# Input x in eight pieces handled ahead of the weights, with idle products on TensorE, in a one-core transformer block

## The reference, cut to what matters

```
h = rmsnorm(x, g_mix);  z = h @ w_in                 # 2048 x 14848 columns in nine groups
o_a = gated linear recurrence (16 heads);  o_b = sliding-window attention (32 heads, 4 key heads)
x = x + concat(sigmoid(gate_a)*o_a, sigmoid(gate_b)*o_b) @ w_out
x = x + square(relu(rmsnorm(x, g_mlp) @ w_up)) @ w_down
x = x + sigmoid(x @ w_ple_gate) * (p @ w_ple_proj)
out = rmsnorm(x, g_final)
```

## Time and profile before

| | |
|---|---|
| median of the runs shown | 1722.49 us |
| the profiled execution's own time | 1721.62 us |
| its span, first to last instruction | 1719.9 us |
| TensorE busy | 1698.4 us, 99% |
| VectorE busy | 1105.5 us, 64% |
| ScalarE busy | 925.2 us, 54% |
| mean rate of the DMAs | 183 GB/s |

### The profile page before, as it was taken

One profiled execution on the slowest core, in us unless ns is written; L12 is line 12 of the kernel. 1 busy time (PEld: TensorE's weight loads), 2 busy tenths in 40 slices (PEclk: granted clock), 3 DMA queues, 4 the chain that ended last, 5 costly groups with the idle time before them and its releaser, 6 DMA issues.

```text
span 1719.9 us, 23521 instructions
## 1 busy us (share of the span) xinstructions
PE 1698.4 (99%) x8685; PEld 1416.6 (82%) x8685; DVE 1105.5 (64%) x1409; ACT 925.2 (54%) x1227; POOL 17.2 (1%) x72
## 2 busy tenths in 40 slices
PE   7999999999999999999999999999999999999997
PEld 6887887788887888878888888888888888888886
DVE  6667866875668756687585565655555556566565
ACT  6566646655566555655546544445454545454454
POOL 3000000000000000000000000000000000000000
PEclk9999999999999999999999999999999999999999
DMA  6665555566655566655556666666666666665654
GB/s 221 204 176 172 173 176 165 172 178 178 184 179 168 179 175 186 178 171 174 180 174 214 184 195 185 195 187 195 191 190 192 190 190 192 188 192 187 183 182 137
DMA packets 163293, 315.35 MB, mean 183 GB/s; under 512 B 10161, under 2 KB 10482, under 8 KB 163058
## 3 DMA queue, kind: packets, MB, share of 16 engines
q1 hardware_dynamic: 162016, 312.01, 60.1%
q10 hardware_dynamic: 1170, 1.87, 0.3%
HBM read 311.74 MB, written 2.10 MB: 182 GB/s over the span
## 4 chain that ended last, share of the span: by engine, by line
PE 96%; ACT 2%; DVE 1%; DMA 0%; issue 0%; SPq 0%; ACTq 0%; DVEq 0%
PE acc L681 21%; PE acc L682 21%; PE acc L687 21%; PE acc L695 6%; PE turn L695 6%; PE turn L682 3%; PE turn L687 3%; PE turn L681 3%; PE turn L701 3%; PE acc L701 3%; PE turn L723 2%; ACT w_hi L982 0%; PE turn L774 0%; ACT pr L1035 0%; PE turn L750 0%; PE turn L821 0%
## 5 line engine op out<-in xcount | busy, mean ns | idle before, releaser
L1339 DVE TENSOR_TENSOR w_lo<-w_raw,w_hi 128x1024 fp32r<-128x1024 f32 x588 | 719.8, 1224 | 562.0 <-ACT w_hi L982 559.3
L982 ACT ACTIVATE w_hi<-w_raw 128x1024 fp32r<-128x1024 f32 x588 | 622.7, 1059 | 705.8 <-PE acc L687 448.3
L681 PE MATMUL acc<-w_hi,hT 128*128 128x512 f32 x1104 | 436.0, 395 | 3.9 <-DVE hT L1379 3.9
L682 PE MATMUL acc<-w_hi,hT 128*128 128x512 f32 x1104 | 431.1, 391 | 0.0
L687 PE MATMUL acc<-w_lo,hT 128*128 128x512 f32 x1104 | 295.4, 389 | 0.0
L681 PEld LDWEIGHTS acc<-w_hi,hT 128*128 128x128 f32 x1104 | 207.9, 188 | 47.8 <-ACT w_hi L982 5.1
L687 PEld LDWEIGHTS acc<-w_lo,hT 128*128 128x128 f32 x1104 | 207.4, 188 | 43.6
L682 PEld LDWEIGHTS acc<-w_hi,hT 128*128 128x128 f32 x1104 | 208.0, 188 | 41.8
L681 PE MATMUL acc<-w_hi,mT_hi 128*128 128x512 f32 x416 | 164.4, 395 | 0.0
L682 PE MATMUL acc<-w_hi,mT_lo 128*128 128x512 f32 x416 | 162.2, 390 | 0.0
L695 PE MATMUL acc<-hT,w_hi 128*128 128x512 f32 x448 | 140.2, 394 | 0.0
(11 more groups left out here) (250 smaller groups left out, 1552.2 us busy)
## 6 DMA issues: line engine op xcount, KB each, us to landing
w_raw<-in_w_in_dram SPq DMA_DIRECT2D x232, 512.0 KB, 3.7
w_raw<-in_w_up_dram SPq DMA_DIRECT2D x128, 512.0 KB, 3.7
w_raw<-in_w_down_dram SPq DMA_DIRECT2D x128, 512.0 KB, 4.6
w_raw<-in_w_out_dram SPq DMA_DIRECT2D x64, 512.0 KB, 3.9
w_raw<-in_w_ple_gate_dram SPq DMA_DIRECT2D x32, 512.0 KB, 4.0
x_sb<-in_x_dram SPq DMA_DIRECT2D x8, 256.0 KB, 7.3
w_raw<-in_w_ple_proj_dram SPq DMA_DIRECT2D x4, 512.0 KB, 4.1
out_dram<-x_sb SPq DMA_DIRECT2D x6, 256.0 KB, 3.1
```

The costliest lines, as they stand in the source:

```text
L681: pe.matmul(a, hi[:, k, t, :], w_hi[:, s, kk, :], start=first and kk == 0, stop=False)
L682: pe.matmul(a, lo[:, k, t, :], w_hi[:, s, kk, :], start=False, stop=False)
L982: act.activation(w_hi[:, n % W_SLOTS], w_raw[:, n % RAW_SLOTS], ACT.Copy)\
L1339: dve.tensor_tensor(w_lo[:, n % W_SLOTS], w_raw[:, n % RAW_SLOTS], w_hi[:, n % W_SLOTS].bitcast(F32), ALU.subtract).then_inc(w_lo_ready, 1)
```

## The change

x comes in eight pieces of 256 columns, both halves of the rows in one DMA of 256 KB (rows of 1 KB). SP sends piece 0 first, then the weights of chunk 0, pieces 1 and 2, the weights of chunk 1, piece 3, and so on. The two small rows move from SP to ACT's queue, so that hgrn_norm_g's row is issued fourth there. TensorE makes five idle products (128 x 128 float32, identity times identity, into a PSUM tile that is free) ahead of its wait for `rows`, and eight more between the turn of piece 0 and chunk 0. Piece 1 is turned in the middle of chunk 0, between the four products of its first 128 rows and the four of its second; piece n+1 ahead of chunk n for n = 1 to 6. The transposes are 32 as before. ACT rounds piece 0 ahead of `w_hi` of chunk 0, and piece n+1 behind `w_hi` of chunk n. DVE weights and subtracts piece 0 ahead of `w_lo` of chunk 0, weights piece 1 behind it, and for n = 1 to 6 weights piece n+1 ahead of `w_lo` of chunk n and subtracts it behind. One piece is as many elements as one (block, t) was: eight operations of each kind, as before.

```diff
+PIECES = 8
+PIECE = D_MODEL // PIECES
...
-            sp.dma_start(rows[0:16, :], g_mix[0]...)
-            sp.dma_start(rows[16:32, :], g_mlp[0]...)
+            def load_x(i):
+                cs = slice(i * PIECE, (i + 1) * PIECE)
+                sp.dma_start(x_sb[:, :, cs], x_rows[:, :, cs]).then_inc(x_landed[i], 16)
             load_x(0)
             for slot in HEAD:
                 load(slot)
-                if slot[0] in (1, 2, 3):
-                    load_x(slot[0])
+                if slot[0] == 0:
+                    load_x(1)
+                if slot[0] + 2 < PIECES:
+                    load_x(slot[0] + 2)
...
# TensorE, in chunk()
+                if kind == "kv":
+                    pe.wait_ge(hT_ready, c + 1)
                 for kk in range(2):
+                    if n == 0 and kk == 1:
+                        pe.wait_ge(x_landed[1], 16)
+                        x_piece_turn(1)
...
+            def idle_products(n):
+                for _ in range(n):
+                    pe.matmul(acc[1][1][:, 0:P], ident[:], ident[:], start=True, stop=True)
             pe.wait_ge(ident_made, 1)
+            idle_products(5)
             pe.wait_ge(rows_landed, 16 * 4)
             pe.transpose(bank(("rows",))[:, 0:P], rows[:], ident[:])
             for slot in HEAD:
-                (two turns ahead of chunks 0, 1, 2 and 4)
+                if n == 0:
+                    pe.wait_ge(x_landed[0], 16)
+                    x_piece_turn(0)
+                    idle_products(8)
+                elif n + 1 < PIECES:
+                    pe.wait_ge(x_landed[n + 1], 16)
+                    x_piece_turn(n + 1)
                 chunk(slot)
...
# ScalarE
+            act.dma_start(rows[0:16, :], g_mix[0]...)
             act.dma_start(rows[32:64, :], lb_logits...)
+            act.dma_start(rows[16:32, :], g_mlp[0]...)
             act.wait_ge(rows_filled, 1)
             act.dma_start(rows[64:65, :], hgrn_norm_g)
...
             for slot in HEAD:
+                if slot[0] == 0:
+                    x_piece_hi(0)
                 split_hi(slot)
-                if slot[0] in (0, 2, 4, 6): (x_hi for t = 0 and 1)
+                if slot[0] + 1 < PIECES:
+                    x_piece_hi(slot[0] + 1)
...
# VectorE
             for slot in HEAD:
-                if slot[0] in (0, 2, 4, 6): (x_weighted for t = 0 and 1)
+                if slot[0] == 0:
+                    x_piece_weighted(0)
+                    x_piece_lo(0)
+                elif slot[0] + 1 < PIECES:
+                    x_piece_weighted(slot[0] + 1)
                 split_lo(slot)
-                if slot[0] in (0, 2, 4, 6): (x_lo for t = 0 and 1)
+                if slot[0] == 0:
+                    x_piece_weighted(1)
+                if slot[0] + 1 < PIECES:
+                    x_piece_lo(slot[0] + 1)
```

More of the change, by code:

```diff
@@ L217, in sem @@
             return ctx.enter_context(nc.semaphore(name))
-        x_landed = [[sem(f"x_landed{t}{cb}") for cb in range(4)] for t in range(TT)]
+        x_landed = [sem(f"x_landed{i}") for i in range(PIECES)]
         rows_filled = sem("rows_filled")
@@ L419, in program @@
         use(("rows",), 3, cols_ready, 1)
-        for cb in range(4):
-            for t in range(TT):
-                use(("xT", cb, t), t + 2 * (cb % 2), tmp_full, 2 * cb + t + 1)
+        for i in range(PIECES):
+            use(("xT", i), i % 4, tmp_full, i + 1)
         for t in range(TT):
@@ L536, in _ @@
         def _(sp):
[L537 to L543, removed]
+            x_rows = x[0].rearrange("(t p) d -> p t d", p=P)
+            def load_x(i):
+                cs = slice(i * PIECE, (i + 1) * PIECE)
+                sp.dma_start(x_sb[:, :, cs], x_rows[:, :, cs]).then_inc(x_landed[i], 16)
             load_x(0)
@@ L674, in chunk @@
                     return
+                if kind == "kv":
+                    pe.wait_ge(hT_ready, c + 1)
                 for kk in range(2):
                     k = 2 * c + kk
+                    if n == 0 and kk == 1:
+                        pe.wait_ge(x_landed[1], 16)
+                        x_piece_turn(1)
                     for t in range(TT):
-                        if kind == "kv" and c % 2 == 0 and kk == 0:
-                            pe.wait_ge(hT_ready, 2 * (c // 2) + t + 1)
                         a = acc_of(kind, j, col, t)[:]
@@ L727, in x_turn, with x_piece_turn @@
                 turn((stage, cb, t), lambda i: x_sb[:, t, (4 * cb + i) * P:(4 * cb + i + 1) * P])
+            def x_piece_turn(i):
+                turn(("xT", i), lambda q: x_sb[:, q % 2, (2 * i + q // 2) * P:(2 * i + q // 2 + 1) * P])
+            def idle_products(n):
+                for _ in range(n):
+                    pe.matmul(acc[1][1][:, 0:P], ident[:], ident[:], start=True, stop=True)
             def head_turn(kind, j, hp, src):
@@ L957, in _ @@
             chain = Chain(act, "act_chain")
+            act.dma_start(rows[0:16, :], g_mix[0].rearrange("(h p) -> h p", p=P)).then_inc(rows_landed, 16)
             act.dma_start(rows[32:64, :], lb_logits.rearrange("a (h p) -> (a h) p", p=P)).then_inc(rows_landed, 16)
+            act.dma_start(rows[16:32, :], g_mlp[0].rearrange("(h p) -> h p", p=P)).then_inc(rows_landed, 16)
             act.wait_ge(rows_filled, 1)
@@ L987, in sum_squares @@
                 for half in range(2):
-                    if stage == 0:
-                        act.wait_ge(x_landed[t][2 * half], 16)
-                        act.wait_ge(x_landed[t][2 * half + 1], 16)
+                    if stage == 0 and t == 0:
+                        for i in range(4 * half, 4 * half + 4):
+                            act.wait_ge(x_landed[i], 16)
                     act.activation(squares, x_sb[:, t, half * 1024:(half + 1) * 1024], ACT.Square,
@@ L1007, in x_hi, with x_piece_hi @@
                    .then_inc(hi_done, 1)
+            def x_piece_hi(i):
+                act.wait_ge(tmp_full, i + 1)
+                act.activation(hT_hi[:, 2 * i:2 * i + 2], tmp[:, i % 2].rearrange("p (k t c) -> p k t c", k=2, t=TT),
+                               ACT.Copy).then_inc(hi_done, 1)
             def z_out(kind, j, dst, done, func=ACT.Copy, scale=R):
@@ L1301, in _ @@
             for slot in HEAD:
+                if slot[0] == 0:
+                    x_piece_hi(0)
                 split_hi(slot)
-                if slot[0] in (0, 2, 4, 6):
-                    for t in range(TT):
-                        x_hi(0, slot[0] // 2, t)
+                if slot[0] + 1 < PIECES:
+                    x_piece_hi(slot[0] + 1)
                 act.wait_ge(w_hi_ready, slot[0] + 1)
@@ L1364, in x_weighted @@
             def x_weighted(stage, cb, t):
-                name = ("xT" if stage == 0 else "x1T", cb, t)
+                name = ("x1T", cb, t)
                 dve.wait_ge(full(name), nth(name))
@@ L1380, in x_lo, with x_piece_weighted, x_piece_lo @@
                                   ALU.subtract).then_inc(hT_ready, 1)
+            def x_piece_weighted(i):
+                name = ("xT", i)
+                dve.wait_ge(full(name), nth(name))
+                if i >= 2:
+                    dve.wait_ge(hT_ready, i - 1)
+                g = cols[:, 2 * i:2 * i + 2].unsqueeze(2).to_broadcast([P, 2, TT * P])
+                dve.tensor_tensor(tmp[:, i % 2].rearrange("p (k c) -> p k c", k=2),
+                                  bank(name)[:].rearrange("p (k c) -> p k c", k=2), g, ALU.mult).then_inc(tmp_full, 1)
+            def x_piece_lo(i):
+                dve.wait_ge(hi_done, i + 1)
+                ks = slice(2 * i, 2 * i + 2)
+                dve.tensor_tensor(hT_lo[:, ks], tmp[:, i % 2].rearrange("p (k t c) -> p k t c", k=2, t=TT),
+                                  hT_hi[:, ks].bitcast(F32), ALU.subtract).then_inc(hT_ready, 1)
             def rotate(src, dsts, t, heads, ta, tb):
@@ L1770, in _ @@
             for slot in HEAD:
-                if slot[0] in (0, 2, 4, 6):
-                    for t in range(TT):
-                        x_weighted(0, slot[0] // 2, t)
+                if slot[0] == 0:
[3 more added lines that the diff above has]
+                    x_piece_weighted(slot[0] + 1)
                 split_lo(slot)
-                if slot[0] in (0, 2, 4, 6):
-                    for t in range(TT):
-                        x_lo(0, slot[0] // 2, t)
+                if slot[0] == 0:
+                    x_piece_weighted(1)
+                if slot[0] + 1 < PIECES:
+                    x_piece_lo(slot[0] + 1)
                 dve.wait_ge(w_lo_ready, slot[0] + 1)
```

## The result

| | before | after |
|---|---|---|
| median of 12 runs each | 1722.78 us (1721.59 to 1725.18) | 1726.29 us (1725.63 to 1729.41) |
| the profiled execution | 1721.62 us, span 1719.9 | 1728.20 us, span 1726.4 |
| ratio, 95% interval | | 1.0023 (1.0016 to 1.0031) |

The forecast was 1721.5 us, in 1718.5 to 1723.7, with 0.04 on slower by over 0.2%. The kernel is slower by 0.23%. The two profiled executions differ by more than the medians (6.6 against 3.5 us): the one of before lies 1.2 us under its median, the one of after 1.9 above. So traces show places, and medians what a place is worth.

A forecast was written before the change was run, and what follows sets the result against it. TensorE, busy 99%, was taken as the bound. Chunk 0 at 9.45 plus 28.35 put chunk 8 at 37.8 against 38.32, gain 0.5: 1721.62 - 0.5 = 1721.1, with half the run's offset 1721.5 us, range 1718.5 to 1723.7.

The forecast's parts named there:

- The likeliest case: Whole kernel: chunk 8 starts at 37.8 against 38.32, gain 0.5, time 1721.5 us; chance 0.47.
- The rows: Start: hgrn_norm_g's row, issued fourth on ACT at 2.28, takes 2.5 and is there at 4.8.
- rival B: Start: the rows land late behind x and the weights, chunk 0 starts 2.2 later, 1723.7 us; chance 0.11.
- S: Start of chunk 0 on TensorE, forecast 9.45 us, set by the idle products, against 11.89 before.
- point of decision: Start: if the rows land at 5.8 or later, the kernel is slower than before.
- The clock: Chunk 0: the clock rises at 9.4, 3.5 us after the eight idle products begin at 5.9; gained 1.6.
- The ties: Chunks 0 to 8: ACT and DVE lose their lead, TensorE waits; 3.92 + 3.17 + 9.96 + 11.3 = 28.35 us.
- restart: TensorE after a stall: restarting its pipeline, bounded by 0 and 0.16 each, 1.3 for eight stalls; taken as 0.
- rival A: Chunks 0 to 8: TensorE runs without gaps, 24.9 us, gain 4.0, 1718.1 us; this or most of it 0.12.
- The loop: Behind the start of chunk 8: nothing is changed, so the two kernels are compared there.
- half carry: Whole time: the profiled run is 0.87 under the median; half is carried over, from 1721.1 to 1721.5.

The follow-up runs named there:

- rows_first: Changed kernel with g_mix's and g_mlp's rows sent by SyncE ahead of x again; 1726.33 us, 1.0021 of the kernel before.
- before_idle: Kernel before with only the 13 idle products added, five ahead of its wait for the rows, eight ahead of chunk 0; 1722.39 us, 0.9996.
- before_8: Kernel before with eight idle products between the first turns and chunk 0, none ahead of the rows; 1721.00 us, 0.9990.
- no_idle: Changed kernel without its 13 idle products; 1727.51 us, 1.0025 of the kernel before.
- lead_rows_8: Changed kernel with small rows sent first, pieces turned one chunk earlier, and only the eight idle products ahead of chunk 0; 1719.45 us, 0.9981 of the kernel before.
- lead_rows_8_late: lead_rows_8 with ScalarE's sums of squares and the three small steps that depend on them one slot later; 1720.92 us, 0.9987 of the kernel before.
- lead_one: Changed kernel with pieces 2 and 3 turned ahead of chunk 1, then piece n+2 ahead of chunk n; 1725.14 us, 1.0013 of the kernel before.
- lead_rows: Changed kernel with small rows sent first and pieces turned one chunk earlier, all 13 idle products kept; 1720.78 us, 0.9988 of the kernel before.
- after_8: Changed kernel without the five idle products ahead of the rows, the eight kept; 1725.42 us, 1.0015 of the kernel before.

## Why the prediction was wrong, step by step

The likeliest case had chunk 8 0.5 us earlier than before; it came 3.7 us later (first records, 41.89 for 38.16). Of its steps:

- **The rows: the largest error of one term.** "I take 2.5: 4.8" was 4.4 us, and TensorE turned the rows at 6.80: 2.0 us late, of which 1.7 show at chunk 0's first record (11.19 for 9.45; by the chain, 11.54, it is 2.1). This is rival B, at nearly its full price (S = 11.7), and its point of decision (a landing at 5.8) held. I gave it 0.11. The reason for 2.5, that "the row is one short line", was wrong: TensorE waits for all four small DMAs, 65 lines, and the change sends them side by side with x and the first weights. The bounds of the term (4.1 to 7.0) held it; the row nearest in kind, a small DMA issued amid x and weights at 2.28, was the sinks' 4.7. rows_first shows the cause. The Trainium skill (DMA: Bandwidth & Descriptors, Queues, rings and completion order) says that each of the 16 engines takes turns between the queue rows that have work. By that rule a small DMA on ScalarE's queue shares its engines with SyncE's backlog; the trace agrees, with 44 packets of q10 beside 452 of q1, and 4.4 us behind a backlog and 1.8 without.
- **The clock.** "It comes at 9.4: chunk 0 is warm" was 12.15 by the trace's clock reading, 4.2 us after the eight began and not 3.5: two of chunk 0's products ran at the low level, 0.3 us by the chain (0.5 by the records, which give that much less to the rows). The mechanism held (before_idle, before_8, no_idle against the changed kernel).
- **The ties: mechanism right, size low.** Chunk 0 to 1 took 4.44 for 3.92 (the clock), 1 to 2 3.34 for 3.17, 2 to 5 10.86 for 9.96, 5 to 8 12.06 for 11.3. The last two are 1.7 us too little. I had DVE start 0.09 after the turn, by the chain; it starts 0.70 after the turn's first record, as in before (17.10 after 16.41), and that is 0.34 after chunk n's first record (22.94 after 22.60). And a stall costs a restart, which I set at 0: chunk 8 takes 2.85 us behind its wait in lead_rows_8 and 2.72 without it in lead_rows_8_late, 0.13 for one stall by the records. By the chain it is 0.27, since the first step behind the wait is 0.50 and not 0.23. The bound was 0.16. The waits are where the prediction put them: w_lo in chunks 2 to 5, w_hi ahead of 6, 7 and 8. lead_one and lead_rows show that they hang on the lead. With the clock up in each from the first or second product, chunks 0 to 7 take 24.7 us in before_8, 25.6 in lead_rows_8 and 30.2 in after_8: the ties cost some 5 us, where the prediction had 3.4 (28.35 less rival A's 24.9).
- **The loop.** "I compare the two kernels at the start of chunk 8, since behind it nothing is changed" failed. The traces lose 2.64 us more at the loop's two turns, about 2 of it against a usual trace; in medians five idle products more are worth 0.9 to 1.4, part of it start. No rival had it. That it depends on the number of idle products ahead of the loop, and not on the x order, the early clock or the size of the program, is shown. That TensorE waits there for instructions that are fetched anew, where a block of them ends at an unlucky place of the loop's head, fits the second gap closely: its end follows the "instruction" packet, and its place moves with the records ahead of it. But no run moved the loop's head by anything else than idle products or looked for the gap at a place named beforehand, so it is argued and not shown. What makes the first gap longer or shorter stays open.

The terms 1.7, 0.5, 0.2, 0.9 and 0.75 add to 4.05, which is the distance of chunk 8 (41.89) from the forecast's 37.8. With 0.9 for the loop they make 5.0, and the median missed the forecast by 4.8 (1726.29 for 1721.5); that these come so close is partly luck, since the terms are of one trace each. The range ended at 1723.7, 2.6 us short: it held B alone and allowed for a restart, but not both with the ties' own error and the loop, all on one side. The half carry of 0.4 had no weight in it.

What the change does well is real: x in pieces, sent first and handled ahead of the weights, with the pieces turned a chunk earlier, the small rows first and the eight idle products alone, makes 1719.45 us, 3.4 under before, of which the idle products alone give 2.0.

## What to carry to other kernels

When work is split finer along a chain of engines, ask who now runs ahead of whom: an engine at 54% is still late if each step waits for one made just in time, and its long jobs then show. Send the smallest transfer that everything waits for first, even if it delays the large one. And when two kernels differ by a fraction of a per cent, match the same instruction in both traces along the whole run: instructions that cost nothing where they stand can cost where the loop turns back. Match against more than one trace of the old kernel: here the single one was 0.4 us early at its start and had the shortest gaps of all at the turns.

## What the runs showed of the hardware that was not expected

- Four small DMAs, 65 lines of 512 bytes, were usable 1.8 us after the last one's issue with nothing large ahead, and 4.4 us behind x and the first weights; the positions took 3.6 and 7.3.
- The clock's rise after unbroken idle or real products began: 3.6 us in before, 4.2 in the changed kernel, 3.7 in lead_rows_8 (from 5.54 to 9.24), 3.6 in before_8 (7.99 to 11.62), but 2.2 in after_8 (8.22 to 10.38).
- A product behind a short wait of TensorE cost 0.13 us beyond the wait by the records (2.85 against 2.72 for a chunk, lead_rows_8 and lead_rows_8_late), 0.27 by the chain.
- With 13 or 15 idle products ahead of a loop its two turns cost 1.9 to 3.3 us more than in the trace of before, with none, 5, 8 or 26 0.4 to 0.9. The difference is one gap within the loop's first chunk, which ends 1.2 to 1.5 us after a 16 KB packet of the "instruction" queue has landed.
